# A hybrid decoder step on one core: two passes over the tokens, with the experts of the first pass's blocks inside the second, and plain fp32 projections

## The reference

```
proj = x @ w_in                                   # 2048 -> z, xbc, dt, u and v, gates
y_a  = ssd_branch(z, conv(xbc), dt, states)       # 8 groups of 8 heads, chunks of 128 tokens
y_b  = gelu(u) * (W_s layer_norm(gelu(v)) + b)    # mixing inside chunks of 128 tokens
merged = g_a * (y_a @ w_branch_a) + g_b * (y_b @ w_branch_b)
h    = layer_norm(ALPHA * x + merged @ w_out)
q    = h @ peer_wq
# 8 heads, each the best 16 of 128 x 128 experts by two top-16 lists; softmax gives the gates
out  = layer_norm(ALPHA * h + sum over the 128 chosen e of gate_e * gelu(h . u_tab[e]) * v_tab[e])
```

## Time and profile before

| | |
|---|---|
| median of 3 runs | 5945.03 us (5941.09 to 5946.6) |
| profiled execution, its own time | 5940.17 us |
| its span, first to last instruction | 5938.7 us |
| mean granted TensorE clock | 0.758 |
| busy: PE | 3107.9 us, 52% |
| busy: PEld | 2921.8 us, 49% |
| busy: DVE | 4166.6 us, 70% |
| busy: ACT | 1050.4 us, 18% |
| busy: POOL | 2935.3 us, 49% |
| moved by DMA | 1431 MB, 241 GB/s over the span |

### The profile page before, as it was taken

The page is one execution under the profiler, slowest core; times in us unless marked ns, Lnnn a source line. Parts: engine busy times, 40 slices in busy tenths (PEclk is TensorE's granted clock), DMA queues, the critical chain, the costliest instruction groups (busy, mean ns, idle before and its releaser), DMA issues. The chain is left out here.

```text
span 5938.7 us, 64797 instructions
## 1 busy us (share of the span) xinstructions
PE 3107.9 (52%) x24030; PEld 2921.8 (49%) x24030; DVE 4166.6 (70%) x4842; ACT 1050.4 (18%) x1322; POOL 2935.3 (49%) x1685
## 2 busy tenths in 40 slices
PE   7999999999999999999986500000000000000000
PEld 7888888889999999999886100000000000000000
DVE  5777777772431223333379699999999999999999
ACT  3333333332322222122221000000000000000000
POOL 1344344440000000000045488888888888878886
PEclk9999999999999999999998555555555555555555
DMA  3333333323223333333120799999999999999998
GB/s 116 103 106 102 102 103 103 101 86 114 80 98 142 115 110 136 132 119 119 57 78 28 295 421 420 421 421 421 421 420 420 421 420 421 420 416 421 420 420 371
DMA packets 209369, 1431.24 MB, mean 241 GB/s; under 512 B 25144, under 2 KB 25528, under 8 KB 46152
## 3 DMA queue, kind: packets, MB, share of 16 engines
q0 software_dynamic: 175088, 1175.67, 48.7%
q1 hardware_dynamic: 34144, 253.53, 11.9%
HBM read 1382.88 MB, written 46.21 MB: 241 GB/s over the span
## 5 line engine op out<-in xcount | busy, mean ns | idle before, releaser
L192 PE MATMUL psum<-acts_hi,w_hi_ring 128*128 128x260 f32 x7168 | 2073.2, 289 | 98.0 <-ACT raw L577 35.0
L193 PE MATMUL psum<-acts_lo,w_hi_ring 128*128 128x260 f32 x7168 | 2039.5, 285 | 0.0
L194 PE MATMUL psum<-acts_hi,w_lo_ring 128*128 128x260 f32 x7168 | 2037.4, 284 | 0.0
L192 PEld LDWEIGHTS psum<-acts_hi,w_hi_ring 128*128 128x128 f32 x7168 | 1366.4, 191 | 128.8 <-issue 95.8
L193 PEld LDWEIGHTS psum<-acts_lo,w_hi_ring 128*128 128x128 f32 x7168 | 1366.4, 191 | 13.7 <-issue 13.7
L194 PEld LDWEIGHTS psum<-acts_hi,w_lo_ring 128*128 128x128 f32 x7168 | 1367.0, 191 | 0.0
L1568 DVE SCALAR_TENSOR_TENSOR acc<-rows,coef,acc 128x2048 f32<-128x2048 f32 x512 | 1204.1, 2352 | 41.3 <-DMA rows<-in_peer_v,expert 12.0
L1554 DVE SCALAR_TENSOR_TENSOR rows<-rows,shared 128x2048 f32<-128x2048 f32 x512 | 1157.9, 2290 | 75.7 <-DMA rows<-in_peer_u,expert 44.9
L1431 POOL DMA_INDIRECT rows<-in_peer_u,expert x512 | 1095.6, 2140 | 222.7 <-issue 154.8
L1431 POOL DMA_INDIRECT rows<-in_peer_v,expert x512 | 1090.4, 2130 | 173.6 <-issue 155.4
L159 DVE TENSOR_TENSOR w_lo_ring<-w_raw,w_hi_ring 128x2048 fp32r<-128x2048 f32 x210 | 501.8, 2390 | 540.1 <-ACT w_hi_ring L153 531.9
(11 more groups left out here) (260 smaller groups left out, 3360.3 us busy)
## 6 DMA issues: line engine op xcount, KB each, us to landing
w_raw<-in_w_tiles SPq DMA_DIRECT2D x224, 1024.0 KB, 4.8
smp_state<-in_state_ssm POOLq DMA_DIRECT2D x64, 256.0 KB, 4.0
out_ssm_sample<-smp_state POOLq DMA_DIRECT2D x64, 256.0 KB, 2.8
branch_in<-branch_acts POOLq DMA_DIRECT2D x12, 1040.0 KB, 12.6
gate_ring<-branch_gates POOLq DMA_DIRECT2D x48, 260.0 KB, 2.9
branch_acts<-shared POOLq DMA_DIRECT2D x8, 1040.0 KB, 5.4
branch_gates<-gate_stage POOLq DMA_DIRECT2D x32, 260.0 KB, 2.3
rows<-in_peer_u,expert POOLq DMA_INDIRECT x512, 25.9
```

What stands on the lines that cost most here:

```text
L192: pe.matmul(o, self.wh[:, j, ks], self.ah[:, k, hs], start=(k == 0), stop=False)
L193: pe.matmul(o, self.wh[:, j, ks], self.al[:, k, hs], start=False, stop=False)
L194: last = pe.matmul(o, self.wl[:, j, ks], self.ah[:, k, hs], start=False, stop=(k == KB - 1))
```

## The change

- Projections are single fp32 matmuls with fp32 weights and activations: no split, no high and low copies. A tile is 16 matmul instructions in each pass (`gemm`). Weights go through a ring of three places.
- There are two passes over the tokens, and each runs through all stages. Pass A has the first two blocks of 128 prompt tokens and the sample's 8 (264 columns), pass B the last two blocks (256 columns). Each pass loads all 224 weight tiles. The convolution's last rows stay in SBUF between the passes, the SSD states go to HBM and come back. Gates stay in SBUF.
- The experts of pass A's two blocks (256 steps, each one u row and one v row per token) run inside pass B: `plan` gives every tile of pass B a number of steps, 262 slots in all with the lag of 6 between a dot and its weighted sum, and `Experts` issues them in program order on VectorE, ScalarE and POOL. Their rings have four u and four v buffers.
- The experts of pass B's blocks, those of the sample and all final norms stand in `tail`, with rings of eight.
- The decoding of the indices moves from POOL to VectorE. The loops are written out: there is no loop instruction left.
- In `ssd` the parameters of all groups are loaded once, the group's norm is put behind the second tile of the next group, and the order of the two chunks' parts is written out for each engine. Stores of the branch inputs and states move from POOL's queue to SP's.

The core of the diff:

```diff
+ORDER = list(range(O_GATE))
+ORDER += [O_GATE + FT + n for n in range(FT)]
+ORDER += [O_GATE + n for n in range(FT)]
+ORDER += [O_BR + 2 * FT + n for n in range(FT)]
+for _n in range(FT):
+    ORDER += [O_BR + FT + _n, O_BR + _n]
+ORDER += list(range(O_OUT, N_TILES))
+P_GB, P_GA, P_WB, P_WA = O_GATE, O_GATE + FT, O_GATE + 2 * FT, O_GATE + 3 * FT
+P_OUT, P_Q = O_OUT, O_Q
+N_GROUPS = N_TILES - FT
...
+RING = 3
+PASSES = 2
+CP = CH // PASSES
+NP = CP * P
...
+    def begin_rows(self, pool):
+        for s in range(self.ring):
+            self.u_row(pool, s)
+        for s in range(self.ring):
+            self.v_row(pool, s)
+    def rows(self, pool, s):
+        self.u_row(pool, s + self.ring)
+        if s - self.lag >= 0:
+            self.v_row(pool, s - self.lag + self.ring)
...
+    def gelus(self, act, s):
+        if s < self.total and s % 4 == 3:
+            q = s // 4
+            c = slice(4 * (q % 2), 4 * (q % 2) + 4)
+            act.wait_ge(self.dot_done, 4 * q + 4)
+            if q >= 2:
+                act.wait_ge(self.coef_done, q - 1)
+            act.activation(self.ge[:, c], self.dots[:, c], ACT.Gelu).then_inc(self.gelu_done, 1)
+    def step(self, dve, s):
+        if s < self.total:
+            self.dot(dve, s)
+        if s >= self.lag:
+            self.add(dve, s - self.lag)
+    def dot(self, dve, s):
+        u = self.urow[s % self.ring]
+        dve.wait_ge(self.u_in[s % self.ring], 16 * (s // self.ring + 1))
+        if s >= 8:
+            dve.wait_ge(self.gelu_done, s // 4 - 1)
+        dve.scalar_tensor_tensor(out=u, in0=u, scalar=1.0, in1=self.k.htok[:, self.blocks[s // P], :],
+                                 op0=ALU.mult, op1=ALU.mult,
+                                 accum_out=self.dots[:, s % 8:s % 8 + 1]).then_inc(self.dot_done, 1)
+    def add(self, dve, k):
+        b, j, q = k // P, k % P, k // 4
+        acc = self.acc[b]
+        if j == 0:
+            dve.wait_ge(self.dot_done, P * b)
+            dve.tensor_scalar(acc, self.k.htok[:, self.blocks[b], :], ALPHA, None, ALU.mult).then_inc(self.acc_set, 1)
+            dve.wait_ge(self.acc_set, b + 1)
+        if k % 4 == 0:
+            c = slice(4 * (q % 2), 4 * (q % 2) + 4)
+            dve.wait_ge(self.gelu_done, q + 1)
+            if k >= 4:
+                dve.wait_ge(self.acc_done, k - 4)
+            dve.tensor_tensor(self.coef[:, c], self.ge[:, c], self.k.gates[:, self.blocks[b], j:j + 4],
+                              ALU.mult).then_inc(self.coef_done, 1)
+            dve.wait_ge(self.coef_done, q + 1)
+        dve.wait_ge(self.v_in[k % self.ring], 16 * (k // self.ring + 1))
+        if k >= 1:
+            dve.wait_ge(self.acc_done, k)
+        dve.scalar_tensor_tensor(out=acc, in0=self.vrow[k % self.ring], scalar=self.coef[:, k % 8:k % 8 + 1],
+                                 in1=acc, op0=ALU.mult, op1=ALU.add).then_inc(self.acc_done, 1)
...
-    def lo(self, dve, n):
-
-        j, n, half = n
-        dve.wait_ge(self.w_hi, n + 1)
-        dve.tensor_tensor(self.wl[:, j, :], self.w_raw[:, j, :], self.wh[:, j, :].bitcast(F32),
-                          ALU.subtract).then_inc(self.w_split, 1)
...
-                pe.matmul(o, self.wh[:, j, ks], self.ah[:, k, hs], start=(k == 0), stop=False)
-                pe.matmul(o, self.wh[:, j, ks], self.al[:, k, hs], start=False, stop=False)
-                last = pe.matmul(o, self.wl[:, j, ks], self.ah[:, k, hs], start=False, stop=(k == KB - 1))
...
+    def load_weight(self, sp, p):
+        if p >= PASSES * N_TILES:
+            return
+        if p >= RING:
+            sp.wait_ge(self.w_used, p - RING + 1)
+        sp.dma_start(self.w_ring[:, p % RING, :],
+                     self.a["w_tiles"][ORDER[p % N_TILES]]).then_inc(self.w_in[p % RING], 16)
+    def gemm(self, pe, p, grp, x, n, start=True, stop=True, x_ready=None):
+        o = self.bank[grp % 2][:, 0:n]
+        if start and grp >= 2:
+            pe.wait_ge(self.free[grp % 2], grp // 2)
+        pe.wait_ge(self.w_in[p % RING], 16 * (p // RING + 1))
+        for k in range(KB):
+            if x_ready:
+                pe.wait_ge(*x_ready(k))
+            last = pe.matmul(o, self.w_ring[:, p % RING, k * P:(k + 1) * P], x[:, k, :],
+                             start=start and k == 0, stop=stop and k == KB - 1)
+        last.then_inc(self.w_used, 1)
...
+    def plan(self):
+        at, s = {}, 0
+        def put(key, n):
+            nonlocal s
+            at[key] = range(s, min(s + n, SLOTS + LAG))
+            s = at[key].stop
+        for g in range(G):
+            for c in range(9):
+                put(("ssd", g, c), 1)
+        for n in range(FT):
+            put(("v", n), 1)
+        for n in range(FT):
+            put(("u", n), 1 + n % 2)
+        for c in range(2 * FT):
+            put(("gate", c), 1 + c % 2)
+        for n in range(FT):
+            put(("wb", n), 1 + (n % 5 in (1, 3)))
+        for n in range(FT):
+            put(("wa", n), 3)
+        for n in range(FT):
+            put(("out", n), 1 + (n % 5 in (1, 3)))
+        put(("ln", 0), 1)
+        put(("ln", 1), 1)
+        for n in range(FT):
+            put(("q", n), 1)
+        put(("end", 0), SLOTS + LAG)
+        return at
...
+                    self.one_pass(passes[0], xs, spare, None)
+                pe = Experts(self, "ea", 4, LAG, list(range(CP)), [acc0[:], self.htok[:, 0, :]])
+                with ExitStack() as st:
+                    rows = gs(st, "rows_a", [P, 2 * pe.ring, D])
+                    pe.place(rows, *(gs(st, n, [P, 8]) for n in ("dots_a", "gelu_a", "coef_a")))
+                    xs = gs(st, "x_acts1", [P, KB, passes[1].n])
+                    self.one_pass(passes[1], xs, late, pe)
+            self.tail(acc0)
...
+                project(0, 0)
+                for g in range(G):
+                    project(g, 1)
+                    if g > 0:
+                        rms(g - 1)
+                    project(g, 2)
+                    if ps.smp:
+                        spread(g, 0)
+                    project(g, 3)
+                    if ps.smp:
+                        spread(g, 1)
+                    project(g, 4)
+                    project(g, 5)
+                    project(g, CT)
+                    chunk_a(g, 0)
+                    project(g, CT + 1)
+                    project(g, CT + 2)
+                    chunk_b(g, 0)
+                    chunk_a(g, 1)
+                    project(g, CT + 3)
+                    if g < G - 1:
+                        project(g + 1, 0)
+                    chunk_b(g, 1)
+                rms(G - 1)
...
+                    conv(g, 5)
+                    tri_rhs(g, 0)
+                    expert(g, 4)
+                    sum_smp(g, 0)
+                    spread_chunk(g, 0)
+                    tri_rhs(g, 1)
+                    sum_smp(g, 1)
+                    expert(g, 5)
+                    weigh(g, 0)
+                    sum_smp(g, 2)
+                    dve.wait_ge(b_done, CP * g + 1)
+                    next_state(g, 0)
+                    outputs(g, 0).then_inc(y_done, 1)
+                    dve.wait_ge(y_done, CP * g + 1)
+                    sum_smp(g, 3)
+                    expert(g, 6)
+                    spread_chunk(g, 1)
+                    sum_smp(g, 4)
+                    expert(g, 7)
+                    weigh(g, 1)
+                    sum_smp(g, 5)
+                    if g < G - 1:
+                        conv(g + 1, 0)
+                    sum_smp(g, 6)
+                    dve.wait_ge(b_done, CP * g + 2)
+                    outputs(g, 1)
+                    next_state(g, 1).then_inc(y_done, 1)
...
```

More of the change, by code:

```diff
@@ L210, in build, with steps, span @@
+    def steps(self, ps, *key):
+        return self.at[key] if ps.i == 1 else ()
+    def span(self, *names):
+        every = [s for key, r in self.at.items() if key[0] in names for s in r]
+        return range(min(every), max(every) + 1)
     def build(self):
@@ L492, in ssd @@
+        st_out = [self.sem(f"s_st_out{j}") for j in range(4)]
         dord, pord = S_("dve", "pool")
@@ new lines, in project, with spread @@
+                def project(g, t):
+                    self.gemm(pe, pos(g, t), grp(g, t), xs, n)
+                def spread(g, m):
+                    pe.wait_ge(diag_ready, 2 * g + m + 1)
+                    pe.wait_ge(root_ready, g)
+                    pe.wait_ge(spread_read, 2 * g + m)
+                    for h in range(2):
+                        last = pe.matmul(ab[h][:], self.ones[:], flat(tri[:, 4 * h:4 * h + 4, :]),
+                                         start=True, stop=True)
+                    last.then_inc(spread_done, 1)
@@ L893, in sgu @@
+            y_out = [self.sem(f"e_y_out{j}") for j in range(CH + 1)]
+            dord, pord = S_("dve", "pool")
+            gather = lambda pool, dst, table, idx: pool.indirect_dma_start(
+                out=dst, out_offset=None, in_=table, in_offset=bass.IndirectOffsetOnAxis(ap=idx, axis=0))
```

(18 more changed lines are left out.)

2107 lines of the change are left out of this document (1018 added, 1089 removed).

## The result

The changed kernel takes 5566.67 us (median of 4 runs, 5560.54 to 5569.94) against 5943.11 for the kernel before in the same comparison: a ratio of 0.9365, interval 0.9349 to 0.9381. It is 6.3% faster. The forecast was 5685 with a range of 5570 to 5890: the direction and the mechanism came as forecast, the size is 118 us short, and the measured time lies 3 us under the range. The profiled execution took 5567.98 us with a span of 5566.1, 112.9 under the forecast's 5679.

A forecast was written before the change was run, and what follows sets the result against it. TensorE bounds some 3290 us, then the experts' gathers 2650. Pass A 2008, pass B 2293 and tail 1378 sum to a 5679 us span, 5685 against the median; range 5570 to 5890.

The forecast's parts named there:

- What bounds the kernel, and what moves: Whole kernel: TensorE, then gathers as limits; half the gathers move under TensorE's work, saving 1272 us in the tail.
- The tile's price: Projections: fp32 tiles of 7.1 us in pass A and 6.9 in pass B, both passes 559 us dearer than before.
- the SSD group: SSD stage, eight groups in each pass: 93 us a group in pass A and 94 in pass B.
- PE's work beside the tiles: SSD matmuls other than projections: 20 us a group in pass A, 16 in pass B.
- VectorE's 83 us in pass B: SSD group of pass B: 41 us of VectorE's own work plus 42 for nine expert steps.
- The 9 us of waits added to PE's 85: SSD group of pass B: three near equal loads leave gaps, so 94 us instead of PE's 85.
- The ends: Bare pieces around SSD: 28 us after pass A's last group; in pass B 13 at the start, 30 at the end.
- Rival 1, the clock: Pass B: PE's idle gaps lower its clock, deciding under a mean grant of 0.57; 6130 us if throughout; chance 7%.
- Rival 2, in-order coupling: Pass B: waits in program order make a group 108 us and 128 later tiles 1 us dearer; 5760 to 5925; 17%.
- Rival 3, mixed DMA: Pass B: gathers and weights together run at only 376 GB/s, 146 us more; 5830 us; chance 10%.
- Rival 4, the gaps close: SSD group of pass B at 88 us, pass A without its 2 us and half its bare pieces; 5580 us; 10%.
- The rule on bandwidth: V to output in pass B: if mixed traffic were held to 358 GB/s, 215 us more, 5900 us in all.

The follow-up runs named there:

- Run 1: Changed kernel with all 256 expert steps of pass A's blocks moved behind pass B's queries, so nothing overlaps: 6413.87 us, ratio 1.0784 to the kernel before.
- run 2: Kernel before, still one pass, with one plain fp32 matmul in place of three fp32r ones, splits still made: 6387.22 us, ratio 1.0739.
- run 3: Changed kernel without pass B's gathers except the first into each row buffer, compute instructions kept: 5226.87 us in one run.
- run 4: Changed kernel loading only half of each weight tile from pass B's fourth V tile on: 5446.18 us in one run.
- run 5: Changed kernel with ten expert steps instead of nine per pass-B SSD group, the seventh ahead of VectorE's wait, 8 fewer steps in branch A: 5526.03 us.
- run 7: Changed kernel, still nine steps, with each pass-B SSD group's seventh expert step put ahead of VectorE's wait for the branch's products: 5545.53 us.
- run 9: Eleven expert steps per pass-B SSD group, against the changed kernel with ten, early seventh step and first gathers behind x's load (5507.02 us): 5490.76 us.
- run 6: Changed kernel with GpSimd waiting for pass B's x before it issues pass B's first gathers: 5549.76 us.

## Why the prediction was right, and where it was short

*What bounds the kernel, and what moves.* Right. Half of the gathers went under TensorE's work and the tail came out at 1373 us for 1378. Run 1 puts the overlap at 847 us, of 1282 that the moved steps take by themselves: two thirds stayed, one third was paid back, three quarters of it in the stage where DMA is the limit.

*The tile's price.* Right where PE is the bound: 2.48 us a tile in run 2, and in pass A V to queries took 977 for 978. In pass B's back stage the forecast took 936 us of DMA and 37 for reloads and hand-overs; 990 were measured. Runs 3 and 4 show that it is DMA that sets them; 140 steps at the 4.94 us of run 5 and 96 tiles at the 2.4 of run 4 are 922, which would leave some 68 for reloads and hand-overs.

*The step that failed: the SSD group.* The forecast said 93 us in pass A and 94 in pass B. The change has 88.2 ((761.4 - 56.0)/8, from the first projection to the last group's products) and 86.5 ((2674.0 - 1982.2)/8):

```profile
55.99 8.34 PE L293 MATMUL psum<-x_acts,w_ring 128*128 128x264 f32 x25 [7.59 <-PEq L253]
...
759.71 1.68 PE L722 MATMUL psum<-spare,b_tok 128*128 128x512 f32 x2
...
1982.25 8.05 PE L293 MATMUL psum<-x_acts,w_ring 128*128 128x256 f32 x27 [29.11 <-DMA x_acts<-in_xT]
...
2672.89 1.12 PE L722 MATMUL psum<-h_tokens,b_tok 128*128 128x512 f32 x2
```

In pass A the eight groups are 39 us shorter than forecast, of the stage's 50; in pass B they are 60 shorter, of which the start took 14 back. In pass A the term is PE's work beside the tiles, 15.1 us a group where 20 were taken. In pass B it is mostly the 9 us of waits added to PE's 85, where some 3 were lost, and PE's other work, 13.2 for 16. The parts:

- PE's work beside the tiles, "the other 287 are 36 a group for four chunks, so 20 for two with the sample's part". The window of the earlier trace rows held 81 tiles, not 80 (2592 matmuls of each of the three products, 32 a tile), so 11 us of the 287 were a tile; why the rest more than halved was not looked into. In the trace after, the projections are 579.9 of pass A's 701.0 us and 559.7 of pass B's 664.9: the other work is 15.1 and 13.2 a group against 20 and 16 forecast. The tiles themselves came out at 7.25 and 7.0 us, for 7.1 and 6.9 forecast, which gives back one us a group or a little more.
- VectorE's 83 us in pass B. "Three near equal loads" were not: it is busy 603.05/8 = 75.4 a group. The forecast took 11 of 92 us for the sample and halved the rest, to 41 for pass B. Without the 72 steps (some 340 us by the lines below, with 6 more of the second kind into the other sum) VectorE has 33, and in pass A 455.65/8 = 57 for the 51 forecast. The sum over both passes was right (90 for 92); its split between them was not. VectorE's 83 us didn't set the forecast, PE's 85 did; they stood for the claim that gaps can't be avoided. VectorE's lines in pass B's SSD:

```profile
L205 DVE SCALAR_TENSOR_TENSOR rows_a<-rows_a,h_tokens 128x2048 f32<-128x2048 f32 x72 | 164.6, 2286 | 1.1
L228 DVE SCALAR_TENSOR_TENSOR acc<-rows_a,coef_a,acc 128x2048 f32<-128x2048 f32 x66 | 154.9, 2347 | 0.6
```

- The 9 us of waits added to PE's 85. The waits were seen rightly (VectorE 4 us in front of the state, PE for the decay behind steps) but they don't all fall on PE, since VectorE had 10 us a group to spare: PE waits 20.5 us for the decayed products in the whole stage, 2.6 a group, and 8.4 for ScalarE. Runs 5, 7 and 9 measure that spare time: the tenth step costs 1.7 of its 4.7 us, the eleventh 3.0.
- The ends. 28 us bare after pass A's last group were 17 to the stage's end at 778. The 13 at pass B's start were 27, with a wait of 29.1 for x, the one part of the stage that was dearer than forecast. The forecast didn't see that the first eight gathers stand beside the load of x; run 6 moves them behind it and gets 19 us of PE's wait back.

*Rival 1, the clock.* It came only in part. In gates to output the granted clock is 0.87, mostly the upper of its two levels (2.4 GHz), and PE is busy 732 of 990 us for work that was put at 662; in run 3, with a grant of 0.98, nearly the same matmuls (3077 for 3103) keep it busy for 669 us. DMA sets this stage (runs 3 and 4), so what the lower clock costs PE there fits into its idle time. A stretch that shows the lower level alone (0.50) is the tail, where PE does nothing. *Rival 2, in-order coupling:* a group of 108 us was too dark; by run 1 the coupling costs SSD 42 us in all, 5 a group. *Rival 3, mixed DMA:* the back stage holds 409 GB/s over all and 418 to 421 in most of its slices, with gathers 73% of the bytes. *Rival 4, the gaps close*, 5580 us at 10%, is what happened, and by more than it said: 86.5 us for 88 in pass B, and in pass A 88.2 for 91. That its sum came within 13 us is partly luck: it took 64 us off the groups and 40 off bare pieces, where the groups gave 99 and the bare ends of the two SSD stages 5 (11 and 8 cheaper, 14 dearer). The fault of the range is that its low end was put beside the one rival that took the work of PE and VectorE as right, and no bound was kept for those two shares, which the trace of before doesn't show by pass.

*The rule on bandwidth.* The tail and the back stage read at up to 421 GB/s again, so the 358 that the prediction weighed didn't bind. The Trainium skill explains this elsewhere ("Perfetto Trace Analysis", Roofline): the 358 GB/s are the share when both cores of a pair are active, and one core alone is held by its 16 DMA engines at about 435. The trace agrees, with 421 GB/s as the highest slice (every run here is of one core). The forecast's fear of a late weight tile (7 us against a cover of 14) is also answered: PE's waits for a weight tile are none in pass B's SSD and one of 12.4 us in gates to output.

## What to carry to other kernels

When a stage is to take more work, ask two questions of it separately: which resource is full (a run without the transfers answers it), and how much room the others have (add one unit of work, then another, and compare each with a kernel that differs in nothing else). Work should leave the stage whose limit it uses and go where that limit is slack, and inside the stage in front of a wait, not behind it. Sizing a stage from a window, count the instructions in it first, and keep a bound of its own for every share that is halved or split by argument.

## What the runs showed of the hardware that was not expected

- The same VectorE instruction was slower in the pass in which GpSimd computes. The convolution's step (128x256, fp32, three sources) takes 709 ns on average in pass A, where POOL forms the sample's products and is busy 430 of 728 us, and 485 ns in pass B, where POOL only issues gathers. VectorE's lines in pass A (busy us, mean ns, idle before):

```profile
L876 DVE SCALAR_TENSOR_TENSOR conv_acc<-raw,g_par,conv_acc 128x256 f32<-128x256 f32 x144 | 102.0, 709 | 5.1
...
L929 DVE TENSOR_TENSOR spare<-spare,cT 128x1024 f32<-128x1024 f32 x16 | 30.2, 1890 | 0.0
```

And in pass B:

```profile
L876 DVE SCALAR_TENSOR_TENSOR conv_acc<-raw,g_par,conv_acc 128x256 f32<-128x256 f32 x144 | 69.9, 485 | 5.1
...
L929 DVE TENSOR_TENSOR h_tokens<-h_tokens,cT 128x1024 f32<-128x1024 f32 x16 | 19.5, 1218 | 0.0
```

  On these two lines alone it is 43 us, 5 a group, and part of why VectorE's work didn't split in half. Inside pass A the step's median is the fast one, and only some are long:

```profile
L876 DVE SCALAR_TENSOR_TENSOR conv_acc<-raw,g_par,conv_acc x144: 483/485/1984, 66.9 to 717.6; 128x256 f32<-128x256 f32 x144
```

  By the timelines of both engines the convolution's steps take some 0.51 us in pass A where POOL computes nothing and 0.97 or more where it does. Issuing gathers doesn't slow them: the mean is 485 ns also in pass B of run 1, where POOL is busy 7 us in all. It doesn't hold for every instruction; L928, of the same size as L929, takes 1308 and 1225 ns. That POOL is the cause is argued from the traces; no run took its work away alone.
- The 2 MB of x are issued 0.8 us before the first of eight gathers of 1 MB, which go to another queue, and land 27.7 us after their issue; with the gathers held back (run 6) they land after 8.8 us. PE waits 29.1 us and 10.2. The order of issue on different queues is no order of service. While both queues have work they move the same number of packets, but those of x's queue are of some 1 KB and the gathers' of some 7, so x's queue gets an eighth of the bytes. The two queues from 1964 to 1979 us (packets, MB, share of the 16 engines):

```profile
q0 software_dynamic: 735, 5.37, 86.9%
q1 hardware_dynamic: 736, 0.80, 15.1%
```

  The prediction's half of the rate for a load beside gathers would need packets of equal size.
- One MB of weights costs 2.4 us of the back stage (an estimate from half tiles) and one MB of gathered rows 2.47 (half a step of 4.94). Gathers alone run at 2.49 in the tail, so beside weights they showed no loss; weights alone were not run at a full DMA.
- Traffic alone cost the compute of SSD almost nothing: with a DMA share of 0.86 and with 0.40 (run 3) the stage ends within 5.4 us.
